# A decoder step on one core: memory rows first, row statistics sooner, low halves of weights by VectorE

## What is computed

```python
def layer(x, ...):
    xn = rmsnorm(x, norm_mix)
    a_b, a_c, a_x, b_val, b_glu, q, gate_logits = jnp.split(xn @ w_in, cuts, axis=-1)
    ya = (a_b * causal_dwconv(buf_a, a_c * a_x, conv_a_w)) @ w_out_a          # width 3
    yb = causal_dwconv(buf_b, b_val * sigmoid(b_glu), conv_b_w)               # width 31
    yb = silu(layernorm(yb + conv_b_bias, ln_b_g, ln_b_b)) @ w_out_b
    yx = softmax(q @ mem_k.T / sqrt(d)) @ mem_v @ w_out_x                     # 4 heads, 256 memory rows
    g = sigmoid(gate_logits + b_gate)
    h = x + (g[0] * ya + g[1] * yb + g[2] * yx) @ w_o
    return h + (silu(rmsnorm(h, norm_ffn) @ w_ff_gate) * (rmsnorm(h, norm_ffn) @ w_ff_up)) @ w_ff_down
# prompt: mem_k, mem_v = rmsnorm(mem) @ w_k, rmsnorm(mem) @ w_v;  results: rmsnorm(layer(...)), mem_k, mem_v, conv states
```

## Time and profile before

| | us |
|---|---|
| median of 3 runs | 1105.8 (1105.73 to 1106.59) |
| the profiled execution | 1104.67 |
| its span, first to last instruction | 1102.9 |
| PE busy | 1086.5 |
| DVE, ACT, POOL busy | 542.3, 490.3, 135.7 |
| granted TensorE clock, mean | 0.996 of 2.4 GHz |

### The profile page before, as it was taken

The page is one execution under the profiler, slowest core; times in us unless marked ns, Lnnn a source line. Parts: engine busy times, 40 slices in busy tenths (PEclk is TensorE's granted clock), DMA queues, the critical chain, the costliest instruction groups (busy, mean ns, idle before and its releaser), DMA issues.

```text
span 1102.9 us, 20964 instructions
## 1 busy us (share of the span) xinstructions
PE 1086.5 (99%) x8987; PEld 1079.8 (98%) x8987; DVE 542.3 (49%) x981; ACT 490.3 (44%) x539; POOL 135.7 (12%) x117
## 2 busy tenths in 40 slices
PE   8999999999999999999999999999999999999997
PEld 8999999999999999999999999999999999999996
DVE  5775677889788664685244432343232332300122
ACT  5744333544334443433447636544444453443331
POOL 3760000002200000000000000000000000000010
PEclk9999999999999999999999999999999999999998
DMA  9947876779886887678776888778777777787762
GB/s 301 281 153 196 219 200 155 224 209 293 251 232 152 188 202 193 159 154 212 167 196 152 205 225 217 173 175 211 188 179 189 181 190 181 174 211 192 188 143 78
DMA packets 135272, 214.80 MB, mean 195 GB/s; under 512 B 4726, under 2 KB 122830, under 8 KB 124566
## 3 DMA queue, kind: packets, MB, share of 16 engines
q0 software_dynamic: 11664, 84.94, 38.6%
q1 hardware_dynamic: 98854, 106.99, 30.2%
q10 hardware_dynamic: 24688, 21.90, 6.4%
HBM read 122.34 MB, written 7.54 MB: 118 GB/s over the span
## 4 chain that ended last, share of the span: by engine, by line
PE 82%; DMA 7%; DVE 5%; ACT 4%; issue 1%; POOL 0%; DVEq 0%; SPq 0%; ACTq 0%
PE acc L1728 51%; PE acc L1744 26%; DMA w_l<-w_raw 4%; PE acc L2069 1%; ACT w_h L557 1%; PE acc L1929 1%; PE acc L1905 1%; DMA w_raw<-in_w_ff_gate_dram 1%; ACT w_l L560 1%; DMA w_raw<-in_w_o_dram 1%; DVE big_l L1041 1%; DMA w_raw<-in_w_k_dram 1%; PE acc L1700 1%; PE acc L2065 1%; DMA stage<-in_mem_prompt_dram 1%
## 5 line engine op out<-in xcount | busy, mean ns | idle before, releaser
L1728 PE MATMUL acc<-big_h,w_h 128*128 128x260 f32 x1960 | 396.3, 283 | 0.8 <-DVE nrm_t L1113 0.4
L1728 PE MATMUL acc<-big_l,w_h 128*128 128x260 f32 x1960 | 393.6, 282 | 0.0
L1728 PEld LDWEIGHTS acc<-big_h,w_h 128*128 128x128 f32 x1960 | 301.3, 188 | 1.7 <-issue 0.9
L1728 PEld LDWEIGHTS acc<-big_l,w_h 128*128 128x128 f32 x1960 | 301.7, 188 | 0.0
L557 ACT ACTIVATE w_h<-w_raw 128x1024 fp32r<-128x1024 f32 x186 | 186.2, 1050 | 170.1 <-PE acc L1728 65.7
L1744 PE MATMUL acc<-big_h,w_l 128*128 128x260 f32 x1960 | 246.2, 282 | 1.1 <-DMA w_l<-w_raw 1.1
L1744 PEld LDWEIGHTS acc<-big_h,w_l 128*128 128x128 f32 x1960 | 239.9, 188 | 1.5 <-DMA w_l<-w_raw 1.4
L1183 DVE SCALAR_TENSOR_TENSOR ubyb<-ubyb,prm 128x512 f32<-128x512 f32 (+1 forms) x240 | 180.3, 751 | 15.6 <-DVE ubyb L1183 9.9
L541 POOL DMA_DIRECT2D w_l<-w_raw x81 | 69.4, 857 | 879.3 <-ACT w_l L560 868.0
L560 ACT ACTIVATE w_l<-w_raw 128x2048 fp32r<-128x2048 f32 x81 | 154.4, 1906 | 25.7 <-PE acc L1744 25.7
L1728 PE MATMUL acc<-hg_h,w_h 128*128 128x260 f32 x704 | 141.8, 283 | 0.0
(11 more groups left out here) (235 smaller groups left out, 821.5 us busy)
## 6 DMA issues: line engine op xcount, KB each, us to landing
w_l<-w_raw POOLq DMA_DIRECT2D x81, 1024.0 KB, 8.1
w_raw<-in_w_in_dram SPq DMA_DIRECT2D x36, 1024.0 KB, 5.4
w_raw<-in_w_ff_gate_dram SPq DMA_DIRECT2D x11, 1024.0 KB, 5.4
w_raw<-in_w_ff_up_dram SPq DMA_DIRECT2D x11, 1024.0 KB, 5.4
k_st<-in_cache_mem_k_dram ACTq DMA_DIRECT2D x8, 1024.0 KB, 7.6
v_st<-in_cache_mem_v_dram ACTq DMA_DIRECT2D x8, 1024.0 KB, 11.1
w_raw<-in_w_ff_down_dram SPq DMA_DIRECT2D x8, 1024.0 KB, 4.9
w_raw<-in_w_v_dram SPq DMA_DIRECT2D x4, 1024.0 KB, 6.4
```

Source lines behind the costliest of these rows:

```text
L1728: last = M.matmul(out[:, b, 0:HALF], w_h[:, slot, k, cols], xs[:, k_at + k, b * HALF:(b + 1) * HALF], start=start and k == 0 and xs is x[0 ...
```

## The change

- SP issues both blocks of memory rows ahead of chunk 0. PE runs 4 more idle transposes after memory rows 0 and 14 after memory rows 1 (`FILL`). ACT makes the high parts of memory rows 0 ahead of the first half of chunk 0, and DVE their low part one place sooner.
- The statistics of batch 2 (`squares` of x rows 2, 3 and the samples, `root(2)`, `mean_rows(2)`, `refine_rows(2)`) move from the round of chunk 2 to the round of chunk 1.
- The low part of the memory's values is read from the accumulator: two SCALAR_TENSOR_TENSOR (`acc * rs - vM[0]`) in place of one subtraction from `kv_f`. So for chunks 4 to 7 the accumulator counts as read only after them; a new semaphore `kv_ready` tells ACT that `kv_f` is there.
- From `OWN` = `C_OB + 1` = 53 on, 41 chunks get their low part by DVE: two subtractions of 128 x 1024 each (`low`), with semaphore `w_own`. ACT's `negative` and POOL's DMA are gone for them, and POOL's subtraction of the last chunk too.
- In `last_rows` the multiplications by the final gain stand ahead of `ssy`, started by a new semaphore `y_flip`; a memset of one column counts the accumulator as read.

```diff
-WARM = 16
+WARM, FILL = 16, (4, 14)
-SUB = (*range(C_B + 2), C_CX + 2, C_CX + 4, C_END - 1)
+SUB = (*range(C_B + 2), C_CX + 2, C_CX + 4)
+OWN = C_OB + 1
@@ SP @@
                 if not isinstance(c, int):
-                    sp.wait_ge(w_rest[slot], turn(c) * 16 - 16)
+                    sp.wait_ge(w_own, own(c) - 4)
+                elif c - 2 >= OWN:
+                    sp.wait_ge(w_own, own(c - 2))
...
             rows(0, mem_prompt[0, 0:P, :])
+            rows(1, mem_prompt[0, P:2 * P, :])
             sp.dma_start(w_raw[:, 0, 0:HK, :], wk[:, 0:HK, 0:CW]).then_inc(w_first, 16)
-            rows(1, mem_prompt[0, P:2 * P, :])
@@ ACT @@
             squares(0, P)
+            memory_hi(0, 0)
+            memory_hi(0, 1)
             act.wait_ge(w_first, 16)
...
-                if c not in SUB:
+                if c not in SUB and c < OWN:
                     done(last_use)
                     negative(slot)
...
-                if c == 2:
-                    for n in (4, 5, 6):
-                        squares(n, TS if n == 6 else P)
-                    root(2)
-                act.wait_ge(acc_read, use + 1)
+                act.wait_ge(*((kv_ready, c - 3) if c >= 4 else (acc_read, use + 1)))
...
                     turned(c - 1)
+                if c == 1:
+                    for n in (4, 5, 6):
+                        squares(n, TS if n == 6 else P)
+                    root(2)
@@ DVE @@
-                ins.then_inc(acc_read, 1)
+                ins.then_inc(kv_ready if c >= 4 else acc_read, 1)
...
+                if c >= 4:
+                    dve.wait_ge(mv_hi, c - 3)
+                    for m in range(2):
+                        ins = V.scalar_tensor_tensor(vM[1][:, m, cols], acc[use % 4][:, m, 0:CW], rs_[:, m:m + 1],
+                                                     f(vM[0][:, m, cols]), ALU.mult, ALU.subtract)
+                    ins.then_inc(acc_read, 1)
...
+            def low(c, used):
+                hi, slot = c if isinstance(c, tuple) else (2 * c, c % 2)
+                dve.wait_ge(*used)
+                for s in range(2):
+                    ks = slice(s * HK, (s + 1) * HK)
+                    dve.wait_ge(w_hi, hi + (s + 1))
+                    V.tensor_tensor(w_l[:, slot, ks, :], w_raw[:, slot, ks, :], f(w_h[:, slot, ks, :]), ALU.subtract) \
+                        .then_inc(w_own, 1)
...
             for n in range(KT):
+                if n % 2 == 0:
+                    low(C_OB + 1 + n // 2, (acc_done, ob(n)))
...
             for p in range(3):
+                for c in range(C_D + 3 * p + 1, C_D + 3 * p + 4):
+                    low_down(c)
...
+            low_down(C_END - 2)
             rows_out(2)
+            low_down(C_END - 1)
...
             def last_rows(use, t, cols):
+                dve.wait_ge(y_flip, 2 if t else 1)
+                for n in (6, 7):
...
                 done(use)
...
-                for n in (6, 7):
...
@@ PE @@
                 flip8(T["mem"] + n, stage[n], P, halfway=mem_flip)
+                for _ in range(FILL[n]):
+                    flip(acc[T["kv0"] % 4][:, 0, 0:P], ident[:, :])
```

107 lines of the change are left out of this document (59 added, 48 removed).

## The result

| | before | changed |
|---|---|---|
| median, us | 1106.19 (4 runs, 1105.73 to 1107.56) | 1099.41 (4 runs, 1098.9 to 1099.76) |
| profiled execution | 1104.67 | 1099.76 |
| its span | 1102.9 | 1098.0 |
| ratio | | 0.9941 [0.9928, 0.9953] |
| the same kernels compared again | 1105.38 (11 runs) | 1100.09 (6 runs), 0.9948 [0.9936, 0.996] |

The change makes the kernel 6.8 us faster in the first comparison and 5.3 in the second. The two profiled executions differ by 4.9 us, not 6.8, and the sum was made for a difference of 4.15. So there are two questions: where the terms were too small, by 0.75 us in all, and where the 1.9 us come from by which the medians differ more than the two profiled executions.

The account below looks back on a forecast made before the run. PE was taken as the bound, busy for 1086.5 of the span's 1102.9 us. Terms 2.2 + 2.2 - 0.8 + 0.55 = 4.15 us off the profiled 1104.67 gave 1100.5, median 1101.65; range 1099.9 to 1103.9.

Parts of the forecast that it names:

- part 4: Low parts by DVE from chunk 53 on: the DMA waits at chunks 53 and 60 go, 2.2 us gained (2.0 to 2.6).
- The carried step: Median 1105.8 is 1.1 us above the profiled execution; the same difference was kept between forecast execution 1100.5 and median 1101.65.
- Part 1: Start of the opening: second memory rows sooner, fills keep full clock, first product at 9.4, chunk 0 ends 1.0 us sooner.
- the fills don't keep the clock: Rival in the opening: clock falls at 8.4 us all the same, about 1.4 of 2.2 us stay: 1102.4; chance 0.13.
- part 2: Statistics one round sooner: PE's 1.7 us wait near 38 us goes, chunk 4 starts at 39.35, not 40.5: 1.15 us gained.
- Part 3: Values' low part from the accumulator: DVE's round shrinks, waits on the weight loads go, 1.0 us gained (0.5 to 1.1).
- Part 5: The end: PE waits 0.8 us for y2 (0 to 1.0); reordered last multiplications gain 0.55 us (0.4 to 0.6).
- Freer: Rival: POOL and DVE don't meet in chunk 3, no wait at y2; 1.0 and 0.8 us more, 1100.0; chance 0.12.
- Chunk 3 pays back: Rival: chunk 3's conversion or POOL's halves come 1.5 to 2 us later, opening gains 0.4: 1103.5; chance 0.11.
- x rows were late: Rival: ACT's moved sums wait for x rows 2 and 3; landing at 34 us gives 1108; slower, chance 0.04.
- DMA wait stayed: Rival: at chunks 53 and 60 ACT's copies or the load end last, waits don't go: 1103.8; chance 0.05.

Follow-up runs that it names:

- the longer run of small products: y2_first without the added transposes, with the 8-column value products of sample heads 2 and 3 issued twice: 1101.7 us, five runs from 1101.6 to 1102.09.
- part 2 undone: Changed kernel with the statistics of batch 2 back in the round of chunk 2: 1099.83 us (5 runs), ratio 0.9949.
- y2_first: Changed kernel with accumulator y2 read ahead of chunk 92's low part on DVE: 1098.74 us (5 runs), ratio 0.9939.
- the 8 transposes between the two groups: y2_first without the added transposes in the opening, with 8 transposes of 128 columns between two groups of ten small products: 1099.95 us.
- gap added: Kernel of part 2 undone, with DVE's eight multiplications for x block 1 split into sixteen, to lengthen PE's gap at 38 us: 1102.7 us (7 runs), ratio 0.9959.
- its half: As gap added, but only four of the eight multiplications split: 1101.96 us (6 runs), ratio 0.9959.
- part 1 alone: Kernel before with memory rows first, the 4 and 14 transposes, and ACT's and DVE's order of the memory's parts: 1103.81 us (12 runs), ratio 0.9982.

## Why the prediction was right and wrong

The direction, the places and the signs were right; the time was 2.2 us too high, 0.5 outside the range. **0.75 us of that are terms, 1.45 are the step from the profiled execution to the median.**

**The step that failed: "The median, 1105.8, is 1.1 above it, and I carry the difference over."** Beside it the steady part's term was mis-sized (part 4 below, 2.2 forecast and 2.98 measured). The carried step took the distance between the profiled execution and the median for a property of the measurement. It is one of the kernel. Before has two places at which the clock may fall at a cost, and DMA waits of 0.9 to 2.5 us. Its profiled execution had its stretch at 8.5 us, where it was free, and of its three further profiles each has one that costs 1.2 to 1.6. The changed kernel has neither the long gap at 38 nor the DMA waits; eight of its eleven executions stand on the lower level, at 1098.9 to 1099.8, and its median lies 0.35 *below* its profiled execution in the first result. 1.1 carried, -0.35 found: 1.45 us. The median of before in that comparison, 1106.19, is higher still, 1.5 above the profiled execution: 4.9 + 1.5 + 0.35 = 6.8. That the stretches make up most of this 1.5 + 0.35 is supported (the table of mean clocks, the levels of the changed kernel's times, the longer run of small products), but not measured piece by piece, since no profile of before came without a stretch. The profile of before named the stretch and its place, but I asked of it only what it cost there, and not why a gap of 1.70 us at 38, as long as the one at 8, had none behind it that time.

**Part 1, 1.0 us:** chunk 0's products started at 9.90 and not 9.4 (9.12 to 9.94 in the profiles with fills), because the transposes of memory rows 0 took 1.90 us, at half pace: the forecast took the full clock that PE had by 5.3 us in one profile for granted, and it came at 4.4 to 7.2. Chunk 1 started 0.46 us sooner; over all profiles about 0.7. That the fills hold the clock was the reason given; without them it held too, and the rival "the fills don't keep the clock" was wrong with it. The 1.0 is no addend of its own: PE's earlier arrival at chunk 3 is already in part 2's 1.15.

**Parts 1 and 2 at chunk 4, 1.15 us:** most steps came out: root ended at 29.26 (29.3 forecast), conversion at 29.45 (29.35), POOL's halves with a collision at 5.74 us (5.75), PE's wait 0.83, no wait for `nrm_o`. Chunk 4 started at 39.73, 0.76 sooner than before and not 1.15, of which 0.46 was there at chunk 1. With part 2 undone no loss was seen. The mistake may be in what it was compared with: without part 2 chunk 4 came as early, with 1.12 us of wait for `nrm_o`, but in an execution whose load of chunk 3 landed early. What the profiles show of part 2 is that it turns the gap of 1.9 us into one of 1.1 in a kernel without the others. The Trainium skill, "SBUF — State Buffer", section "Who interferes with whom", was weighed for this place: the trace agrees, since POOL took 5.74 us for its two halves beside DVE's subtraction with two SBUF inputs (4.78 undisturbed, in the row at 15.39 us), and DVE's values' form with an input from PSUM took 0.88 for two at 47.70, where POOL's halves stayed at 2.4 us each.

**Part 3, 1.0 us:** 1.2 in the traces, 1.5 in the medians. The forecast took 1.0 out of its range of 0.5 to 1.1. It did not see that the DVE wait at 519 us goes as well (0.35). From chunk 4 on the opening gained 1.15 (28.65 to 27.50), and that made good what part 1 lacked. Opening in all: 1.91 against 2.2.

**Part 4, 2.2 us:** 2.98. The mechanism was right, with the low part ready 11 us ahead. The size was read from the idle time, 1.15 and 1.02. But matmuls of 260 columns start every 0.12 us while each is listed with 0.28, so the idle column leaves out the time by which an instruction would have overlapped with its neighbour: start to start the two gaps were 1.43 and 1.30 us, 0.12 of each being the pace, thus 2.49 us. The rest, 0.49, are small waits, of which the one at 519 us (0.35) belongs to part 3. This was the largest term that was mis-sized.

**Part 5, -0.8 + 0.55:** PE's wait for y2 was there, in its place, 0.38 us listed and 0.54 start to start: -0.6 with y2_first's 0.64 beside it. The reordered multiplications gave 0.64 (reciprocal 0.43 us after the sums, 1.07 before). Together 0.0 instead of -0.25.

**The range.** The bounds of the four terms in the sum (0.7 to 3.1, 2.0 to 2.6, -1.0 to 0, 0.4 to 0.6) add up to 1099.5 to 1103.7, not to the 1100.0 to 1103.4 that the prediction gives. Even so added, 1099.41 lies below.

**The rivals.** "Freer", 1100.0, was nearest in time, and its mechanism wrong: POOL and DVE did meet, y2 was waited for. "Chunk 3 pays back" was half true for part 2, but part 3 paid for it. No x rows were late (the sums ran at once, the last ended at 28.63), no DMA wait stayed.

## What to carry to other kernels

Before one profiled execution is set against a median, look at the granted clock: where a kernel's times fall into levels, the profile belongs to one, and a change can move the share of executions on each, by removing a gap of PE or a run of tiny matmuls, beside what its own waits cost. Size a wait of a pipelined engine by the distance from start to start less the pace, not by the idle column. And undo each part of a change alone: two things done here (the fills, the statistics) showed no gain when they were undone, and the low parts by DVE cost 0.6 us at the end that exchanging two calls gave back.

## What the runs showed of the hardware

- **A stretch of half clock lasts 3.4 us, and executions of one kernel differ in it.** What decides is not shown here. The same kernel, instruction for instruction, has it or not: the changed kernel 1099.03 to 1099.2 in three runs and 1100.97 to 1101.13 in three.
- **PE needn't stand still for it.** 20 matmuls of 8 columns, in 2.1 us in which the profile calls PE busy throughout, were followed by 1.2 GHz in 6 of 19 profiles, and 36 of them, 3.9 us, in the one profile, with all five times on that level. The Trainium skill, "TensorE: Matmul & The Clock Gate", Part 4, says that transposes don't count as PE being busy the same way. By that rule the 8 transposes between the two groups could not help, and they did not: two of five runs on the upper level. Transposes alone had brought PE to full pace at 5 us, and in all twenty profiles ahead of the first product, though, so the runs show both sides and don't settle the rule.
- **Gaps of PE ahead of the first product did not lower the clock** in the four kernels without fills (2.1 to 2.2 us start to start), and in one of six profiles with the old start (1.0 to 1.9 us) it fell behind them, at 8.5 us, while gaps of 1.8 to 2.2 us at 38 us had half clock behind them in 5 of 8 profiles. What makes the difference stays open.
- **What stays open besides:** where in the other executions of before the costly stretches stand. Four profiles of it show one each, at 8.5, 40.0, 41.1 and 334.6 us. Its times up to 1107.8 would fit two in one execution, which the profiles of gap added and of its half show, but none of before does. Three more executions of it, beside part 1 alone, lie at 1109.7, 1110.0 and 1112.3 us; nothing here explains them. And why part 1 alone, with the gap at 38 in place, had a mean clock of 0.998 in seven of twelve runs isn't explained.
